# Column-interleaved split weights with a strided moving operand, in three stages of a two-block transformer kernel

## The reference

```
first block:   proj = rms_norm(x) @ w_in;  kv = rms_norm(mem) @ w_mem_kv
               (gated linear attention, forgetting attention, memory attention)
               h = x + (o * gate) @ w_out                                <- stage "wout"
               h = h + relu(rms_norm(h) @ w_up)**2 @ w_down
second block:  z = rms_norm(x) @ w_in   (sparse attention, pool mixer)
               y = (g_a * (a @ w_br_attn) + g_p * (p @ w_br_pool)) @ w_mix_out   <- "mixo"
               x = x + rms_norm(y)
               k, v = split(rms_norm(mem) @ w_xkv)                       <- k is stage "xk"
               q = rms_norm(x) @ w_xq ;  x = x + rms_norm(attention(q, k, v) @ w_xo)
               x = x + rms_norm((silu(h @ w_gate) * (h @ w_up)) @ w_down)
```

## Time and profile before

| | us |
|---|---|
| median of 3 runs | 2790.05 |
| lowest, highest | 2789.76, 2791.3 |
| span of the profiled execution | 2789.8 |
| TensorE busy in it | 2673.8 (96%) |
| VectorE busy | 1593.4 (57%) |
| ScalarE busy | 1209.9 (43%) |

### The profile page before, as it was taken

The page is one execution under the profiler, slowest core; times in us unless marked ns, Lnnn a source line. Parts: engine busy times, 40 slices in busy tenths (PEclk is TensorE's granted clock), DMA queues, the critical chain, the costliest instruction groups (busy, mean ns, idle before and its releaser), DMA issues.

```text
span 2789.8 us, 32433 instructions
## 1 busy us (share of the span) xinstructions
PE 2673.8 (96%) x12218; PEld 2204.1 (79%) x12218; DVE 1593.4 (57%) x1976; ACT 1209.9 (43%) x1491; POOL 65.1 (2%) x63
## 2 busy tenths in 40 slices
PE   7999979999999999999999987999999999999997
PEld 6888767688888888878888865878778888888886
DVE  5555776556555555655555456567465555555555
ACT  5433354444444444444333344345554444444443
POOL 0000241000000000000000000000000000000000
PEclk9999979999999999999999999999999999999998
DMA  7666406455556565555555511565455565655652
GB/s 275 182 196 195 139 1 209 138 187 189 182 185 196 188 189 194 188 173 166 196 189 192 153 61 51 192 207 179 140 180 187 191 195 184 192 181 195 195 189 97
DMA packets 248757, 482.67 MB, mean 173 GB/s; under 512 B 17208, under 2 KB 18504, under 8 KB 248040
## 3 DMA queue, kind: packets, MB, share of 16 engines
q1 hardware_dynamic: 239840, 468.25, 52.0%
q0 software_dynamic: 2672, 9.61, 1.0%
q10 hardware_dynamic: 6168, 3.76, 0.5%
HBM read 479.46 MB, written 2.13 MB: 173 GB/s over the span
## 4 chain that ended last, share of the span: by engine, by line
PE 92%; DVE 4%; ACT 2%; issue 1%; ACTq 0%; DMA 0%; DVEq 0%
PE ps_a L2016 24%; PE ps_a L2017 24%; PE ps_a L2018 24%; PE ps_b L2016 5%; PE ps_b L2017 5%; PE ps_b L2018 5%; PE ps_b L2081 1%; ACT prob L940 1%; PE ps_b L2324 1%; DVE wlo L1155 0%; PE ps_a L2434 0%; DVE prob L1786 0%; PE ps_b L2192 0%; PE ps_b L2402 0%; PE ps_b L2424 0%
## 5 line engine op out<-in xcount | busy, mean ns | idle before, releaser
L1155 DVE TENSOR_TENSOR wlo<-raw,whi 128x1024 fp32r<-128x1024 f32 x880 | 1068.9, 1222 | 844.1 <-ACT whi L534 842.5
L534 ACT CAST whi<-raw 128x1024 fp32r<-128x1024 f32 (+1 forms) x884 | 920.5, 1050 | 1184.7 <-PE ps_a L2018 935.9
L2016 PE MATMUL ps_a<-whi,xhi 128*128 128x512 f32 x2592 | 1022.1, 394 | 24.4 <-issue 10.3
L2017 PE MATMUL ps_a<-wlo,xhi 128*128 128x512 f32 x2592 | 1015.3, 392 | 0.0
L2018 PE MATMUL ps_a<-whi,xlo 128*128 128x512 f32 x2592 | 1014.7, 391 | 0.0
L2016 PEld LDWEIGHTS ps_a<-whi,xhi 128*128 128x128 f32 x2592 | 491.0, 189 | 131.5 <-issue 19.9
L2018 PEld LDWEIGHTS ps_a<-whi,xlo 128*128 128x128 f32 x2592 | 490.5, 189 | 102.9
L2017 PEld LDWEIGHTS ps_a<-wlo,xhi 128*128 128x128 f32 x2592 | 491.1, 189 | 100.1
L2016 PE MATMUL ps_b<-whi,uhi 128*128 128x512 f32 x608 | 238.0, 391 | 2.4 <-DVE ulo L1647 2.4
L2017 PE MATMUL ps_b<-wlo,uhi 128*128 128x512 f32 x608 | 237.6, 391 | 0.0
L2018 PE MATMUL ps_b<-whi,ulo 128*128 128x512 f32 x608 | 237.5, 391 | 0.0
(11 more groups left out here) (328 smaller groups left out, 1525.6 us busy)
## 6 DMA issues: line engine op xcount, KB each, us to landing
raw<-in_w_in SPq DMA_DIRECT2D x108, 1024.0 KB, 5.2
raw<-in_w_up SPq DMA_DIRECT2D x108, 1024.0 KB, 5.2
raw<-in_w_down SPq DMA_DIRECT2D x108, 1024.0 KB, 5.1
raw<-in_w_gate SPq DMA_DIRECT2D x44, 1024.0 KB, 5.1
raw<-in_w_out SPq DMA_DIRECT2D x16, 1024.0 KB, 5.2
raw<-in_w_mix_out SPq DMA_DIRECT2D x16, 1024.0 KB, 5.2
raw<-in_w_mem_kv SPq DMA_DIRECT2D x8, 1024.0 KB, 11.6
raw<-in_w_br_attn SPq DMA_DIRECT2D x8, 1024.0 KB, 5.4
```

The lines of the kernel that those rows point to most:

```text
L534: return nc.scalar.copy(o, i)
L1155: return V.tensor_tensor(wlo[:, q % 4], raw[:, c % SLOTS, 2 * j:2 * j + 2], whi[:, q % 4].bitcast(F32), ALU.subtract).then_inc(lo_done, 1)
L2016: mm(o, x0, w0[:, j], start=first and j == 0, stop=False)
L2017: mm(o, x0, w1_[:, j], start=False, stop=False)
```

## The change

In the three stages the 512 columns of each row block of `whi` and `wlo` are stored in another order. With n streams (2 in `wout`, 32 in `mixo`, 256 in `xk`), column i is stored at place (i mod n) * (512/n) + i // n. TensorE reads the places in such an order that the columns come out in their natural order, so PSUM and everything behind it is as before. The three walks step through memory differently:

- `wout`, 2 streams: the reader alternates between two runs that lie 256 floats (1 KB) apart.
- `mixo`, 32 streams: each next column lies 16 floats (64 bytes) on, 32 times, then the walk starts again one float further.
- `xk`, 256 streams: each next column lies 2 floats (8 bytes) on, 256 times, then once more from the second float.

ScalarE writes `whi` along that walk. VectorE reads `whi` and writes `wlo` along it, and reads `raw` straight. For both, the single instruction over 1024 elements becomes two of 512, one for each row block, and only the second raises the semaphore.

```diff
+        STREAMS = {"wout": 2, "mixo": 32, "xk": 256}
+
+        def streams_of(q):
+            names = list(seg)
+            for name, streams in STREAMS.items():
+                if seg[name][1] <= q < seg[names[names.index(name) + 1]][1]:
+                    return streams
+            return 1
+
+        def walked(v, streams):
+            return v if streams == 1 else v.rearrange("p (a b) -> p b a", a=streams)
@@ hi (ScalarE)
+                    n = streams_of(q)
+                    if n > 1:
+                        for m in range(2):
+                            ins = copy(walked(whi[:, q % 4, m], n), raw[:, c % SLOTS, 2 * j + m].rearrange("p (b a) -> p b a", a=n))
+                        return ins.then_inc(hi_done, 1)
@@ lo (VectorE)
+                    n = streams_of(q)
+                    if n > 1:
+                        for m in range(2):
+                            ins = V.tensor_tensor(walked(wlo[:, q % 4, m], n), raw[:, c % SLOTS, 2 * j + m].rearrange("p (b a) -> p b a", a=n),
+                                                  walked(whi[:, q % 4, m], n).bitcast(F32), ALU.subtract)
+                        return ins.then_inc(lo_done, 1)
@@ half (TensorE)
-                        mm(o, x0, w0[:, j], start=first and j == 0, stop=False)
-                        mm(o, x0, w1_[:, j], start=False, stop=False)
-                        ins = mm(o, x1, w0[:, j], start=False, stop=last and j == len(kbs) - 1)
+                        m0, m1 = (walked(w[:, j], streams_of(q)) for w in (w0, w1_))
+                        mm(o, x0, m0, start=first and j == 0, stop=False)
+                        mm(o, x0, m1, start=False, stop=False)
+                        ins = mm(o, x1, m0, start=False, stop=last and j == len(kbs) - 1)
```

## The result

| | before | after |
|---|---|---|
| median, us | 2789.91 | 2893.88 |
| lowest to highest | 2789.52 to 2791.3 | 2889.85 to 2901.33 (4 runs) |
| profiled execution | | 2896.59 |

The account below looks back on a forecast made before the run. TensorE, busy for 96% of the span, was taken as the bound. 2789.8 + 149 (half rate in `wout` and `mixo`) + 0 (`xk`) + 2 (ScalarE, VectorE) = 2941 us, range 2787 to 3030.

Parts of the forecast that it names:

- In these stages a nanosecond on a matmul's pitch counts in full: In the changed stages TensorE is nearly always busy, 99.65 of 102.0 us in `wout`, so longer matmuls lengthen the kernel fully.
- `mixo`, half rate, +74 us: In `mixo`, TensorE's 64-byte step halves its rate, +0.20 us for each of 370 matmuls.
- the factor of 1.57: VectorE's slowdown per element at a 64-byte SBUF step; applied to TensorE's pitch it gives +0.13 us a matmul.
- the extra time of VectorE's row: VectorE's 0.60 ns more an element at a 64-byte step; for TensorE's 512 columns +0.31 us a matmul.
- Each column there too lies far from the one before, so I give it the price of `mixo`: In `wout`, TensorE's two runs in turn were priced at half rate, +0.20 us for each of 376 matmuls.
- Rival 2: Milder TensorE price in `wout` and `mixo`, 2889 us, or only one pays half rate, 2866; put at 2875, chance 0.17.
- rival 4: Every step halves TensorE's rate, `xk` as well: +19 us more, 2960 us, chance 0.12.
- For `xk` I take 0, as L1489 shows: In `xk`, TensorE's 8-byte step was taken as free because a VectorE instruction reading every second float ran at straight speed.
- ScalarE and VectorE, +2 us, bounds +1 to +5: Split, stepping casts and subtractions in the three stages are mostly hidden behind TensorE, showing only in a few waits.
- At half rate TensorE covers it: At the openings of `wout` and `mixo`, slowed TensorE hides VectorE's added work, 2 x 0.67 us a period.
- the period of 6.34 us: TensorE's time at the opening for two halves and one group of turns; VectorE's work would grow from 5.0 to 6.4.
- By that rule VectorE would pay nothing: If odd strides do not slow two-input float32 operations, VectorE's steps are free, changing the sum by under 1 us.

Follow-up runs that it names:

- experiment 1: Changed kernel, but ScalarE and VectorE store whi and wlo straight with one instruction a half; only TensorE's walk kept: 2883.53 us, ratio to before 1.0332.
- experiments 3 and 5: Kernel before, stored straight, with TensorE walking single column tiles in two sets of different orders: 0.216 to 0.487 us a matmul; no total time given.

## Why the prediction was right, and where it was wrong

The direction, the range and the engine were right: TensorE's reader pays and sets the time. 2893.88 lies in 2787 to 3030, 47 us below the forecast of 2941 and outside its own range of 2920 to 2965. That the range holds it owes much to its width: of the two stages that the sum let pay only one did, the stage that it let go free paid, and these errors partly cancel.

1. **"In these stages a nanosecond on a matmul's pitch counts in full"**: right for `mixo` and `xk` (experiment 1, where the pitch alone makes the kernel some 88 us slower, the small matmuls left out).
2. **`mixo`, half rate, +74 us**: right in size and mechanism. The stage grew by 76.5 us and the pitch is 0.433 us, where 0.43 was written. That the factor of 1.57 and the extra time of VectorE's row enclosed it was luck in part: VectorE's own step costs 1.06 against 0.69 us, a factor of 1.54, TensorE's 1.91. A half is no floor either: other walks take 0.451 to 0.487 us.
3. **`wout`, "Each column there too lies far from the one before, so I give it the price of `mixo`", +75 us**: this is the step that failed. Distance does not count: two streams come back to the same two lines and cost 0.216 us at any distance from 16 bytes to 1 KB, 0.011 below straight, about -4 us for the stage. Rival 2 had named it ("two runs in turn may stay at hand for the reader") and gave 2866 us; with rival 4's +19 beside it that would have been 2885.
4. **`xk`, "For `xk` I take 0, as L1489 shows", 0 us**: failed as well, measured +20.1, where rival 4 had +19. The row was right for VectorE (0.689 us in `xk` as predicted) and was carried over to another engine. Two floats of a line were two hits for VectorE and one pair for TensorE. The rule weighed in the prediction ("Advanced Engine Details and Errata", section "SBUF Cachelines", in the Trainium skill: 16 bytes a line, two hits wanted) holds in its line size, by experiments 3 and 5. What it calls a hit it does not say. I took it to be one float, and on TensorE that fails twice: `xk` has two floats of each line in a row and pays, `wout` changes the line with each column and does not. A hit that is a pair of columns fits both.
5. **ScalarE and VectorE, +2 us, bounds +1 to +5**: too low by the opening of `wout`. "At half rate TensorE covers it" hung on step 3: with TensorE at full rate in `wout`, nothing covered. The prediction had worked out that VectorE's load would just reach the period of 6.34 us, with 3.8 us for two halves of `wlo`; at 1.129 us for each of four instructions these were 4.5, so 7.1 in all. 7.0 us of `wlo` came on the chain, ScalarE's casts as well, and "TensorE would wait no more than now for `wlo`" was wrong: the stage has 4 us more idle time and a clock of 0.94 against 0.98. With the shorter pitch and its later start `wout` came out at some +7. ScalarE's cast has 1.06 us in `mixo`, where 0.6 to 0.9 was written: the upper bound, 0.31 us above the straight 0.61 of one cast, was passed by 0.15, since half the extra had been taken without a row.
6. **"By that rule VectorE would pay nothing"** (in the Trainium skill, "VectorE: DVE Perf Modes", section "Mode 1× (REGULAR) — the baseline", which gives one result per cycle and says that weird strides work; that they cost nothing was read from this): the runs decide against it for steps of 16 bytes and more (1.96 to 2.03 us against 1.22 per 1024), as L1754 had hinted.

The profiled execution's span lies 46 us under the forecast. By the steps: `wout`'s pitch -79 (-4 for +75), `mixo` +2.5, `xk` +20, the waits for ScalarE and VectorE +9 (`wout`'s +7 and the 4 that its pitch gave back make 11, where 2 were forecast), the stage after `wout` -3, the 64 small matmuls +5, together -45.5.

## What to carry to other kernels

Take the price of an access pattern from a row of the same engine: one walk was free for VectorE and halved TensorE, another the reverse. On TensorE ask first whether two pairs of columns in a row use the same 16-byte lines (between two lines and eight in turn the answer is a price in between), on ScalarE and VectorE whether two elements in a row do. If a permuted order is wanted, give it to the read side of instructions that exist anyway and leave the stored data straight.

## What the runs showed of the hardware that I had not expected

- A matmul of 512 float32r columns is not at its floor when it reads straight: 0.227 us against 0.216 with two streams, at any distance from 16 bytes to 1 KB. Over the kernel this is worth 106 us (ratio 0.9605).
- TensorE reads two lines in turn at full speed. With four streams it takes 0.27 to 0.28, with eight 0.48 to 0.49 us, more than with 16 or 64 (0.43). Why is not shown.
- VectorE and ScalarE gain nothing from two lines in turn: 2.10 and 2.07 us per 1024, as much as any long step, and writing costs as much as reading. An 8-byte step costs VectorE nothing and ScalarE 0.05 us (1.10 against 1.05), and reading PSUM at it is free for both (684 against 683 ns, 683 against 686).
- 64 small matmuls late in the sparse attention take 7.36 us at a granted clock of 1.00 and 11.5 to 13.9 us at 0.62 to 0.50, from kernel to kernel, which alone moves a run by up to 6.5 us.
